# A mixture-of-experts scatter split in two: first rows written plainly with their residual, second rows added

## The chip, the cores and the metric

One NeuronCore of one Trainium2 chip runs the whole program. The metric is the device time of one execution in microseconds (us); the median of three executions is given. The profile is of one more execution. Engines: PE (TensorE), DVE (VectorE), ACT (ScalarE), POOL (GpSimd), and SP, which here only issues DMAs.

## The reference, cut to what matters

All of it is float32. 1072 tokens (16 meta, 1024 prompt, 32 sample) pass a mixer, and then the part that the change touches:

```python
def channel_mixer(x, norm_g, ...):
    n = rms_norm(x, norm_g).reshape(B * T, D)          # x / sigma * g
    return x + hier_moe(n, ...).reshape(B, T, D)

def hier_moe(h, ...):                                  # 4 groups of 8 experts
    # each token: one group, the 2 best experts in it, two gates
    # rows are sorted by expert, in blocks; for each block of one expert e:
    return (silu(xb @ w_gate[e]) * (xb @ w_up[e])) @ w_down[e]
    # out[token] += gate * that row, for both rows of the token
```

An expert has three float32 matrices of 2 MB each (1024 x 512 twice, 512 x 1024), so the 32 experts together read 192 MB from HBM.

## The kernel before

**Stages.** After the attention part come the out-projection with the residual (`xmid`, nine tiles of up to 128 tokens, `wsteps`), the norm of each tile (`norm_scale`: DVE multiplies by 1/sigma and by the gain `gffn`, into `xg`, which SP stores to `n_scr` in HBM), the router in three batches of tiles (`mark`, `shift`, `sum_gates`, `name_gates`, `name_rows`, `place_slots`), and the store of the residual to `y_all`. The router's result is a table `tab` (96 slots x 32 experts, token numbers; an empty slot names a number past the last token, which an indirect DMA skips) and `gtab` (the gates in the same places). They are products of one-hot matrices on PE (`tables`, `last_tables`), with small filler products (`keep_warm`) where PE would stand idle.

**Expert blocks.** Block b is one expert with up to 96 rows (CAP). POOL gathers its rows from `n_scr` into `xg[b % 2]` (`gather`). For b = 0 and 1 PE transposes them and ACT and DVE copy the halves to `xeT` (`block_left`, `block_right`); later blocks are turned by twelve DVE transposes (`turn_rows`). PE makes gate and up products (`gate_up_product`, line 2827), ACT the silu, DVE the product (`hidden`) and its turn (`turn_hidden`), PE the down product (`down_product`). ACT and DVE write gate times product to `yo[b % 2]` (`left_rows`, `right_rows`), and POOL adds the 96 rows to `y_all` with one accumulating indirect DMA (`scatter`). `moved` makes POOL wait until that scatter and the next gather have landed. The last block (expert 23) is scattered in two halves (`scatter_half`). Rows past 96 of an expert would go to further blocks, which run only if there are any (`count_overflow`, `resume_*`, `further_*`).

**Weights.** A ring of 22 halves of 1 MB (`at_half`; half a matrix each) is filled before the blocks start, as the memory of earlier stages comes free. The 22nd, behind the other tensors, is issued once the router's counts are read. From then on SP walks a fixed list (`asked`): `load_behind` waits until PE has used a half of the ring (`s_gp` or `s_dp`), and issues the next half into it. A block uses six halves.

**Order.** Each engine's instructions stand in a fixed order, written out by hand. In `block_pe(b)` PE makes gate and up of b + 1 and then down of b; `block_dve(b)` is `hidden(b+1)`, `right_rows(b)`, `turn_hidden(b+1)`, `turn_rows(b+3)`; `block_act(b)` is `silu(b+1)`, `left_rows(b)`; POOL's round is `gather(b+3)`, `scatter(b)`, `moved(b)`.

Of the kernel before, what the change touches and what calls it, by code (L numbers as in the profile page):

```python
# [93 lines left out]
def hybrid_step(nc, x_prompt, x_sample, cache_k, cache_v, state_pool, page_table, meta_tokens,  # L94
# [167 lines left out]
    at_half = [at + half_size * half for at in at_ring for half in range(2)] + [at_c, at_q + 4 * size]  # L262
# [15 lines left out]
    assert at_x2 == at_half[-1]  # L278
# [17 lines left out]
    xeT.append(tns)  # L296
    assert at <= at_t

    gffn, at = place("gffn", [P, D], F32, at_u)
# [4 lines left out]
    def table(at, limit, shapes):  # L304
# [10 lines left out]
        ("rhs", [P, 2, NB, 2 * NE], F32), ("prod", [P, 2, NB, NE], F32),  # L315
# [5 lines left out]
    def slot_tables(q):  # L321

        lo, n = BATCHES[q][0], BATCHES[q][1] - BATCHES[q][0]
        if q < 2:
            return row_oh[:, :, 0:n, :], rhs[:, :, 0:n, :]
        at = lo - BATCHES[2][0]
        return late_oh[:, :, at:at + n, :], late_rhs[:, :, at:at + n, :]

# [15 lines left out]
    gcol = [gcols[:, i:i + 1] for i in range(2)]  # L344

# [231 lines left out]
    s_lrg = sem("last_rows_gain_ready")  # L577
# [13 lines left out]
    s_gn = sem("last_gates_named_then_counts_read")  # L591
# [63 lines left out]
    tab_ps = bank[0:CAP, 7, 0:2 * NE]  # L655
# [79 lines left out]
    expert_of = list(range(NE))  # L735
    expert_of[NE - 1 - EPG], expert_of[NE - 1] = NE - 1, NE - 1 - EPG
    assert expert_of[NE - 1] // EPG != expert_of[NE - 2] // EPG

    def scatters(b):

        return 16 * (b + 1) if type(b) is int and b < NE - 1 else 16 * (b + 2)

    def copies(b):

        return scatters(b) // 16 if type(b) is int else b + 2
# [69 lines left out]
    def used(b, half):  # L815

        return 8 * b + 4 * half + 4

# [32 lines left out]
    with nc.allow_non_contiguous_dma(reason="small vectors and broadcasts"), blk as block:  # L851

        @block.sync
        def _(sp):
# [177 lines left out]
            sp.dma_start(gffn[:, :], norm_ffn.to_broadcast([P, D])).then_inc(s_wr, 16)  # L1032
# [92 lines left out]
        def _(pool):  # L1125
# [86 lines left out]
            chain.link(pool.memset(lg[:, LAST, :], 0.0))  # L1212
            pool.wait_ge(s_wr, 64)
# [20 lines left out]
            def rows_named(b, further):  # L1234

                return (tab[:, expert_of[b]:expert_of[b] + 1] if b < NE else further[b % 2][:, 0:1]).bitcast(U32)

            def gather(b):
# [3 lines left out]
                if b >= 2:  # L1242
                    pool.wait_ge(s_xt if b < 4 else s_xc, b - 1)
                pool.indirect_dma_start(out=xg[i][0:CAP, :], out_offset=None, in_=n_scr,  # L1244
                                        in_offset=bass.IndirectOffsetOnAxis(ap=rows_named(b, gidx), axis=0),
                                        bounds_check=T - 1, oob_is_err=False).then_inc(s_gl[i], 16)

            def scatter(b):
# [3 lines left out]
                if b >= NE:  # L1252
                    pool.wait_ge(s_sx2, b - NE + 1)
                pool.indirect_dma_start(out=y_all,  # L1254
                                        out_offset=bass.IndirectOffsetOnAxis(ap=rows_named(b, sidx), axis=0),
                                        in_=yo[b % 2][:, :], in_offset=None, compute_op=ALU.add,
# [8 lines left out]
            r = ROWS[LAST]  # L1265
            pool.wait_ge(s_nst[0], 16 * (LAST // 2))
            pool.wait_ge(s_xm, tile_done(LAST))
            xs, gs = [a.rearrange("r (p k) -> r p k", p=P)[:, P // 2:P, :] for a in (xmid[0:r, LAST, :], gffn[0:r, :])]
            pool.tensor_tensor(xg[0][0:r, :].rearrange("r (k p) -> r p k", p=P)[:, P // 2:P, :], xs, gs, ALU.mult).then_inc(s_lrg, 1)
# [7 lines left out]
            gather(2)  # L1277
# [37 lines left out]
        def _(act):  # L1315
# [312 lines left out]
            def root_mid(t):  # L1628
                r, c = ROWS[t], slice(t % 2, t % 2 + 1)
                act.wait_ge(s_ssq2, t + 1)  # L1630
                act.activation(rs[0:r, c], ss[0:r, c], ACT.Sqrt, bias=eps_col[0:r, 0:1],
# [11 lines left out]
            def scale_last_rows():  # L1643

                r = ROWS[LAST]
                act.wait_ge(s_lrg, 1)
                act.wait_ge(s_lg, NT)
                act.activation(xg[0][0:r, :], xg[0][0:r, :], ACT.Copy, scale=rs[0:r, 0:1]).then_inc(s_n2, 1)
# [14 lines left out]
            act.activation(rs[0:r, 0:1], ss[0:r, 0:1], ACT.Sqrt, bias=rest, scale=1.0 / D).then_inc(s_rms2, 1)  # L1663
# [4 lines left out]
            def block_left(b, i):  # L1668
# [6 lines left out]
                act.activation(xeT[i][:, 0:KT // 2, :], xT_ps[:, 0:KT // 2, 0:CAP], ACT.Copy).then_inc(s_xe, 1)  # L1675
# [7 lines left out]
            def left_rows(b, i):  # L1683

                act.wait_ge(s_dp, 8 * b + 8)
                if type(b) is not int:
                    act.wait_ge(s_gc, b - NE + 1)
                gates = gates_of(b, i)
                since(act, s_sc, 16 * b - 16 if type(b) is int else 16 * b)
# [5 lines left out]
            def last_wide_rows(b):  # L1695

                act.wait_ge(s_sc, 16 * b - 16)
# [5 lines left out]
            def first_act():  # L1703
                for b in range(2):
                    block_left(b, b)
                silu(0, 0)

            def block_act(i, b):
                silu(b + 1, 1 - i)
                left_rows(b, i)  # L1710

            def last_act(b):
                if b == NE - 2:
                    silu(b + 1, 1)
                    left_rows(b, 0)
# [15 lines left out]
        def _(dve):  # L1731
# [329 lines left out]

            def place_slots(q):
# [12 lines left out]
            def gain_last(ps):  # L2075

                r = ROWS[LAST]
                return dve.tensor_tensor(xg[0][0:r, :].rearrange("r (k p) -> r p k", p=P)[:, ps, :],
                                         xmid[0:r, LAST, :].rearrange("r (p k) -> r p k", p=P)[:, ps, :],
                                         gffn[0:r, :].rearrange("r (p k) -> r p k", p=P)[:, ps, :], ALU.mult)  # L2080

# [869 lines left out]
```

## Time and profile before

| | |
|---|---|
| median of three executions | 1090.45 us (1090.32 to 1090.7) |
| the profiled execution, its own time | 1091.88 us |
| its span, first to last instruction | 1090.1 us |
| granted TensorE clock, mean | 0.988 of full speed |
| busy: PE, DVE, ACT, POOL | 96%, 50%, 28%, 16% of the span |
| HBM read, written | 272.98 MB, 42.87 MB |

Busy time is an average over stages. The expert blocks run from about 554 us to the end, half of the span. The "DMA" line of the page gives the mean busy share of the 16 DMA engines in 40 slices of 27.25 us; a window's "DMA share" is the same for a chosen stretch.

### The profile page before, as it was taken

To read this page: it belongs to the slowest core of one execution; us is meant where nothing else is said; L and a number is where in the kernel's file an instruction comes from. 1 tells how busy PE (TensorE), PEld (TensorE's weight loads), DVE (VectorE), ACT (ScalarE), POOL (GpSimd) and SP (SyncE) were. 2 spreads that over 40 slices of the span, in tenths; PEclk is the share of its full clock that TensorE was granted. 3 is DMA by queue.
4 is the path that set the end of the run, shared out by engine and by line. 5 is a ranking of instruction groups with operands and counts; after the bars stand their busy time and mean duration, and the time that the engine had idled before them with its cause. 6 is when DMAs were issued, how large, how long until landed. Compare 5 with 4: busy or idle time off the path is not lost.

```text
span 1090.1 us, 29226 instructions
## 1 busy us (share of the span) xinstructions
PE 1045.2 (96%) x12774; PEld 826.0 (76%) x12774; DVE 544.4 (50%) x1052; ACT 309.3 (28%) x592; POOL 174.6 (16%) x160
## 2 busy tenths in 40 slices
PE   8999999999999999999999999999999988898996
PEld 7999999966666549899876898756898556565665
DVE  5327654378875543444734544555455534343431
ACT  6323332266775552222411011101110111101011
POOL 1001200599200000100010111111111111111102
PEclk9999999999999999999989999999999999999999
DMA  7356785000116467767899999999999999999994
GB/s 244 109 166 211 217 272 155 1 13 2 40 31 211 146 232 251 245 220 277 312 351 393 379 383 385 386 383 375 386 379 382 379 390 388 392 390 389 390 389 111
DMA packets 85816, 293.19 MB, mean 269 GB/s; under 512 B 13425, under 2 KB 44849, under 8 KB 60069
## 3 DMA queue, kind: packets, MB, share of 16 engines
q1 hardware_dynamic: 78277, 273.30, 67.2%
q0 software_dynamic: 7280, 17.58, 6.8%
q8 instruction: 103, 1.69, 0.6%
q10 hardware_dynamic: 128, 0.39, 0.1%
q14 instruction: 28, 0.23, 0.1%
HBM read 272.98 MB, written 42.87 MB: 290 GB/s over the span
## 4 chain that ended last, share of the span: by engine, by line
PE 73%; DMA 18%; DVE 4%; SPq 2%; ACT 1%; issue 1%; POOL 0%; ACTq 0%; POOLq 0%
PE bank L2827 20%; DMA w_all<-in_w_up 18%; PE bank L2375 12%; PE bank L2612 8%; PE bank L2418 4%; PE bank L2844 4%; PE bank L2584 3%; PE bank L2547 3%; PE bank L2848 3%; PE bank L2456 3%; SPq L1042 2%; PE bank L2852 2%; DVE keep L1887 1%; PE bank L2693 1%; PE bank L2479 1%
## 5 line engine op out<-in xcount | busy, mean ns | idle before, releaser
L2827 PE MATMUL bank<-w_all,xeT 128*32 128x256 f32 x6144 | 345.6, 382 | 22.2 <-DMA w_all<-in_w_up 19.2
L2827 PEld LDWEIGHTS bank<-w_all,xeT 128*32 128x32 f32 x6144 | 254.4, 111 | 107.0 <-issue 27.9
L2202 DVE STREAM_TRANSPOSE xeT<-xg 32x256 f32<-32x256 f32 x360 | 156.5, 435 | 97.0 <-DMA xg<-n_scr,tab 91.8
L2844 PE MATMUL bank<-w_all,hT 128*32 128x256 f32 x744 | 165.6, 379 | 0.0
L2848 PE MATMUL bank<-w_all,hT 128*32 128x512 f32 x744 | 129.3, 592 | 0.0
L1887 DVE TENSOR_TENSOR_SCAN keep<-keep,unseen 128x1024 f32<-128x1024 f32 (+7 forms) x64 | 94.8, 1514 | 37.8 <-ACT keep L1439 37.7
L2375 PE MATMUL bank<-w_hi,xh 128*128 128x256 f32 x376 | 108.1, 287 | 0.0
L2375 PE MATMUL bank<-w_hi,xl 128*128 128x256 f32 x376 | 105.5, 281 | 0.0
L2375 PE MATMUL bank<-w_lo,xh 128*128 128x256 f32 x376 | 105.5, 280 | 0.0
L2844 PEld LDWEIGHTS bank<-w_all,hT 128*32 128x32 f32 x744 | 81.8, 110 | 30.3
L1681 ACT ACTIVATE sgl<-bank 128x384 f32<-128x384 f32 x32 | 15.7, 490 | 304.2 <-PE bank L2827 304.2
L2612 PE MATMUL bank<-wo_hi,cat 128*128 128x256 f32 (+1 forms) x384 | 89.0, 321 | 0.4 <-issue 0.4
L1254 POOL DMA_INDIRECT out_y_all<-yo,tab x31 | 44.4, 1432 | 204.9 <-ACT yo L1692 199.8
L2852 PE MATMUL bank<-w_all,hT 128*32 128x256 f32 x744 | 76.4, 379 | 0.0
L1244 POOL DMA_INDIRECT xg<-n_scr,tab x32 | 31.5, 986 | 264.4 <-issue 243.3
L2375 PEld LDWEIGHTS bank<-w_hi,xh 128*128 128x128 f32 x376 | 70.8, 188 | 0.6 <-issue 0.2
L2375 PEld LDWEIGHTS bank<-w_hi,xl 128*128 128x128 f32 x376 | 71.1, 189 | 0.0
L2375 PEld LDWEIGHTS bank<-w_lo,xh 128*128 128x128 f32 x376 | 70.8, 188 | 0.0
L2612 PEld LDWEIGHTS bank<-wo_hi,cat 128*128 128x128 f32 x384 | 64.2, 189 | 5.6 <-issue 0.7
L2234 DVE TENSOR_SCALAR yo<-bank,gtab 96x256 f32<-96x256 f32 x31 | 14.9, 480 | 105.3 <-PE bank L2844 105.3
L2215 DVE TENSOR_TENSOR hid<-sgl,bank 128x384 f32<-128x384 f32 x32 | 27.3, 852 | 77.2 <-PE bank L2827 63.3
L1690 ACT ACTIVATE yo<-bank,gtab 96x512 f32<-96x512 f32 x31 | 21.1, 682 | 144.8 <-PE bank L2844 144.8
(307 smaller groups left out, 1505.9 us busy)
## 6 DMA issues: line engine op xcount, KB each, us to landing
w_all<-in_w_down SPq DMA_DIRECT2D x64, 1024.0 KB, 30.2
w_all<-in_w_gate SPq DMA_DIRECT2D x64, 1024.0 KB, 32.6
w_all<-in_w_up SPq DMA_DIRECT2D x64, 1024.0 KB, 8.9
k_scr<-in_cache_k SPq DMA_DIRECT2D x32, 256.0 KB, 3.3
v_scr<-in_cache_v SPq DMA_DIRECT2D x32, 256.0 KB, 3.5
pgk<-k_scr SPq DMA_DIRECT2D x32, 256.0 KB, 3.9
w_raw<-in_w_in SPq DMA_DIRECT2D x7, 1024.0 KB, 7.1
pgv<-v_scr SPq DMA_DIRECT2D x4, 1024.0 KB, 6.6
```

The source lines that it names most:

```text
L1254: pool.indirect_dma_start(out=y_all, out_offset=bass.IndirectOffsetOnAxis(ap=rows_named(b, sidx), axis=0), in_=yo[b % 2][:, :], in_offset= ...
L1887: dve.tensor_tensor_scan(back, back, unseen[:, NK - w:NK][:, ::-1], 1.0, ALU.mult, ALU.max).then_inc(s_p, 1)
L2202: last = dve.transpose(xeT[i][rows_of(s), :, rows_of(g)], lane[:, :, s, :])
L2375: last = pe.matmul(proj_ps(s)[0:r, :], a[:, k, row0(t):row0(t) + r], b[n % 2][:, k, :], start=(k == 0 and j == 0), stop=(k == KT - 1 and j ...
L2418: last = pe.matmul(wide_ps(s)[:, 0:cols], a[n % 2][:, k, c:c + P], b[:, k, lo:lo + cols], start=(k == 0 and j == 0), stop=(k == KT - 1 and ...
L2456: last = pe.matmul(z_ps(a)[:, lo:lo + n], qT[rows, hp, row0(t):row0(t) + P], kT[rows, hp, lo:lo + n], start=True, stop=True)
L2547: last = pe.transpose(t_ps(n)[0:keys, k, :], keep_of(u, a)[:, P * i:P * i + keys], ident[:, :])
L2612: last = pe.matmul(out_ps(s)[0:r, :], cat_tile(a, t)[:, k, 0:r], b[n][:, k, :], start=(k == 0 and j == 0), stop=(k == KT - 1 and j == 2))
L2827: lasts = [pe.matmul(pair_ps(i)[rows_of(q), g, :, :], xeT[i][:, k, rows_of(g)], pair_of(b, i, k, q), start=(k == 0 and g != 1), stop=(k == ...
L2844: return pe.matmul(y_right_ps(g), hT[:, ft, rows_of(g)], w[ft // 2][:, ft % 2, DA:D], start=first and g != 1, stop=ends, skip_group_check= ...
L2848: pe.matmul(y_left_ps[rows_of(g), :], hT[:, ft, rows_of(g)], w[ft // 2][:, ft % 2, 0:512], start=first, stop=ends, skip_group_check=True)
L2852: lasts = [pe.matmul(y_mid_ps[rows_of(g), :], hT[:, ft, rows_of(g)], w[ft // 2][:, ft % 2, 512:DA], start=first, stop=ends, skip_group_che ...
```

## The change

Each token has two expert rows. The one whose expert stands first in the order of the blocks is now written to `y_all` plainly, by a DMA without accumulation, with the token's residual inside; the second is added as before. For that:

- `norm_scale` no longer applies the gain, so that `n_scr` holds x / sigma. The gain is applied when the rows have been turned: by ACT and DVE in the copies of blocks 0 and 1, and by eight ACT instructions per later block (`gains`). The DVE and POOL instructions that put the gain on the last tile (`gain_last` and one of POOL) go.
- sigma is kept (`sig`), and a third table `wtab` holds sigma in the slots of first rows and 0 in those of second rows (`name_residuals` on DVE, `residual_tables` on PE, `result_tables` on DVE). `result_tables` also makes the two lists of tokens, `tab_first` and `tab_later`.
- `keep_rows` (ACT) writes wtab times the gathered row to the block's result buffer, which is x for a first row and 0 for a second; `add_rows` (DVE, five instructions that read it and PSUM) takes the place of `left_rows` and `right_rows`.
- Each block up to the 31st has two indirect DMAs of 96 slots, one for each list. There are three result buffers; the third lies where the 22nd half of the ring was, so the ring has 21 halves.
- `gather` runs one block further ahead (b + 4), and waits for `keep_rows` of two blocks before. Expert 31 moves to its natural place; 23 stays last.
- 14 fillers before the first block become 8, the residual products, and 4.

```diff
-    at_half = [at + half_size * half for at in at_ring for half in range(2)] + [at_c, at_q + 4 * size]
+    at_half = [at + half_size * half for at in at_ring for half in range(2)] + [at_c]
...
+    yo.append(place("yo2", [CAP, D], F32, at_x2)[0])
+    NY = len(yo)
...
-            sp.wait_ge(s_gn, 2)
-            b, j, half = halves[2 * NWS + 1]
-            load_half(j, expert_of[b], b, b % 2, half)
...
+                if 2 <= b < NE:
+                    pool.wait_ge(s_ya, b - 1)
...
+                else:
+                    pool.indirect_dma_start(out=y_all,
+                                            out_offset=bass.IndirectOffsetOnAxis(ap=column(tab_first, b), axis=0),
+                                            in_=results_of(b), in_offset=None,
+                                            bounds_check=T - 1, oob_is_err=False).then_inc(s_sc, 16)
...
             for b in range(NE - 1):
-                if b + 3 < NE:
-                    gather(b + 3)
+                if b + 4 < NE:
+                    gather(b + 4)
                 scatter(b)
...
-                act.activation(xeT[i][:, 0:KT // 2, :], xT_ps[:, 0:KT // 2, 0:CAP], ACT.Copy).then_inc(s_xe, 1)
+                for k in range(KT // 2):
+                    last = act.activation(xeT[i][:, k, :], xT_ps[:, k, 0:CAP], ACT.Copy, scale=gain_p[:, k:k + 1])
+                last.then_inc(s_xe, 1)
+
+            def gains(b, i):
+
+                act.wait_ge(s_xc, b + 1)
+                for k in range(KT):
+                    last = act.activation(xeT[i][:, k, :], xeT[i][:, k, :], ACT.Copy, scale=gain_p[:, k:k + 1])
+                last.then_inc(s_xe, 1)
+
+            def keep_rows(b, i):
+
+                act.wait_ge(s_gl[i], 16 * (b // 2 + 1))
+                if b < NY:
+                    act.wait_ge(s_tab, 1)
+                else:
+                    act.wait_ge(s_sc, scatters(b - NY))
+                act.activation(results_of(b).rearrange("r (p k) -> r p k", p=P), xg[i][0:CAP, :].rearrange("r (k p) -> r p k", p=P),
+                               ACT.Copy, scale=wtab[:, expert_of[b]:expert_of[b] + 1]).then_inc(s_ya, 1)
...
             def first_act():
                 for b in range(2):
                     block_left(b, b)
+                for b in range(2):
+                    keep_rows(b, b)
                 silu(0, 0)
+                gains(2, 0)
 
             def block_act(i, b):
                 silu(b + 1, 1 - i)
-                left_rows(b, i)
+                if b + 2 < NE - 1:
+                    keep_rows(b + 2, i)
+                if b + 3 < NE:
+                    gains(b + 3, 1 - i)
...
+            def add_rows(b, i):
+                dve.wait_ge(s_dp, 8 * b + 8)
+                dve.wait_ge(s_ya, b + 1)
...
+                add(slice(0, CAP), slice(0, 512), y_left_ps)
+                add(slice(0, CAP), slice(512, DA), y_mid_ps)
+                for g in range(LANES):
+                    last = add(rows_of(g), slice(DA, D), y_right_ps(g))
+                last.then_inc(s_yd, 1)
...
                 for b in range(2):
                     block_right(b, b)
+                result_tables()
                 count_overflow()
...
-            keep_warm(14)
+            keep_warm(8)
+            pe.wait_ge(s_gn, 3)
+            residual_tables()
+            keep_warm(4)
```

## Rows read from the trace of the kernel before

**Rows 1.** The page: DMA busy tenths in 40 slices of 27.25 us.
```profile
DMA  7356785000116467767899999999999999999994
```
**Rows 2.** Windows: busy us of PE, PEld, DVE, ACT, POOL; PEclk, DMA share, GB/s.
```profile
545.00:552.00 7.00, 7.00 (x38) 6.87 (x38) 1.06 (x4) 0.00 (x0) 2.56 (x4) 0.53 0.71 241
552.00:560.00 8.00, 7.70 (x119) 5.85 (x118) 0.56 (x1) 0.49 (x1) 1.00 (x1) 0.99 1.02 419
...
750.00:800.00 50.00, 50.00 (x852) 39.30 (x847) 23.82 (x50) 7.30 (x14) 8.16 (x7) 1.00 1.02 384
...
850.00:900.00 50.00, 43.27 (x706) 26.95 (x698) 22.70 (x48) 6.12 (x12) 5.79 (x5) 1.00 1.02 385
```
**Rows 3.** The chain that ended last: start us, us, what.
```profile
548.13 5.29 PE bank L2769 x28
...
554.38 5.39 PE bank L2827 x96
...
581.44 10.36 PE bank L2827 x192
...
814.53 10.14 PE bank L2827 x188
...
1060.65 10.57 PE bank L2827 x192
```
**Rows 4.** SP's DMA issues around the first release: start us, us.
```profile
549.72 0.81 SPq L1042 DMA_DIRECT2D w_all<-in_w_down  x1
559.88 0.33 SPq L1042 DMA_DIRECT2D w_all<-in_w_gate  x1
```
**Rows 5.** All 192 weight loads (line 1042), issue to landing.
```profile
DMA to landing us min/median/max: 5.9/31.3/35.7
```
**Rows 6.** DMA queues, packets, MB, share: 728:734, 759:764, then 598:602 us.
```profile
q0 software_dynamic: 112, 0.36, 30.0%
...
q0 software_dynamic: 112, 0.21, 21.2%
...
q1 hardware_dynamic: 178, 1.29, 87.7%
q0 software_dynamic: 112, 0.20, 15.9%
```
**Rows 7.** DMA queues: ACT's queue (q10) in 536:543, the loads' (q1) in 538:539 us.
```profile
q10 hardware_dynamic: 128, 0.39, 14.1%
...
q1 hardware_dynamic: 34, 0.26, 62.8%
```
**Rows 8.** The page: the queue of POOL's DMAs over the whole span.
```profile
q0 software_dynamic: 7280, 17.58, 6.8%
```
**Rows 9.** Timeline of DVE: start us, us, instruction, idle before it.
```profile
548.24 0.19 DVE L2163 COPY gtab<-bank 96x32 f32<-96x32 f32 x1 [2.33 <-PE bank L2749]
...
564.32 0.17 DVE L2176 CAST ovmi<-ovm 1x23 int32<-1x23 f32 x1
...
581.56 0.48 DVE L2234 TENSOR_SCALAR yo<-bank,gtab 96x256 f32<-96x256 f32 x1 [3.74 <-PE bank L2844]
```
**Rows 10.** Timeline of ACT.
```profile
535.16 1.15 ACT L1648 ACTIVATE xg<-xg,rs 48x1024 f32<-48x1024 f32 x1 [0.85 <-DVE lg L2109]
...
553.79 0.49 ACT L1675 ACTIVATE xeT<-bank 128x384 f32<-128x384 f32 x1 [10.10 <-PE bank L2800]
...
581.56 0.68 ACT L1690 ACTIVATE yo<-bank,gtab 96x512 f32<-96x512 f32 x1 [4.67 <-PE bank L2844]
582.26 0.95 ACT L1692 ACTIVATE yo<-bank,gtab 32x256 f32<-32x256 f32 x2
```
**Rows 11.** Groups: busy us, mean ns, idle before and what ended it.
```profile
L2202 DVE STREAM_TRANSPOSE xeT<-xg 32x256 f32<-32x256 f32 x360 | 156.5, 435 | 97.0 <-DMA xg<-n_scr,tab 91.8
```
**Rows 12.** Timeline of POOL at the end: line 1254 `scatter`, line 1295 `scatter_half`.
```profile
1078.99 1.40 POOL L1254 DMA_INDIRECT out_y_all<-yo,tab  x1 [14.39 <-ACT yo L1692]
...
1083.09 1.40 POOL L1295 DMA_INDIRECT out_y_all<-yo,lidx  x1 [0.55 <-issue]
```

More of the change, by code:

```diff
@@ L1276, in _ @@
                 pool.tensor_scalar(lidx[:, part:part + 1], tab[:, e:e + 1], 2.0, float(part), ALU.mult, ALU.add).then_inc(s_ln, 1)
-            gather(2)
+            for b in range(2, 4):
+                gather(b)
             pool.wait_ge(s_yst, 16 * LAST)
@@ L1662, in _ @@
             act.wait_ge(s_ssq2, NT)
-            act.activation(rs[0:r, 0:1], ss[0:r, 0:1], ACT.Sqrt, bias=rest, scale=1.0 / D).then_inc(s_rms2, 1)
+            act.activation(sig[0:r, LAST:NT], ss[0:r, 0:1], ACT.Sqrt, bias=rest, scale=1.0 / D).then_inc(s_rms2, 1)
             act.dma_start(y_all[row0(LAST):T, :], xmid[0:ROWS[LAST], LAST, :]).then_inc(s_yl, 16)
@@ L1714, in last_act @@
                     silu(b + 1, 1)
-                    left_rows(b, 0)
                 else:
@@ L2060, in name_rows, with name_residuals @@
                 chain.done(dve.tensor_tensor(slot_tables(q)[1][:, :, :, 0:NE], ek[:, :, 0:n, :], rows, ALU.mult))
+            def name_residuals(q):
+                lo, hi = BATCHES[q]
+                ts, n = slice(lo, hi), hi - lo
+                if q == 2:
+                    dve.wait_ge(s_tbp, 2)
+                places = tmp32[:, 0:n, 0:2 * EPG].rearrange("p t (k e) -> p k t e", k=2)
+                numbers = io_row[:, 0:EPG].rearrange("p (x y e) -> p x y e", x=1, y=1).to_broadcast([P, 2, n, EPG])
+                chain.link(dve.tensor_tensor(places, oh[:, :, ts, :], numbers, ALU.mult))
+                chain.link(dve.reduce_sum(turn[:, :, ts], places, axis=AXX))
+                for k in range(2):
+                    chain.done(dve.tensor_tensor(weight[:, k, ts], turn[:, k, ts], turn[:, 1 - k, ts], ALU.is_lt))
+                chain.settle()
+                chain.link(dve.tensor_tensor(weight[:, :, ts], weight[:, :, ts],
+                                             sig[:, ts].rearrange("p (x t) -> p x t", x=1).to_broadcast([P, 2, n]), ALU.mult))
+                return dve.tensor_tensor(residual_table(q), ek[:, :, 0:n, :], each(weight[:, :, ts], NE), ALU.mult)
             def place_slots(q):
@@ L2146, in _ @@
                         chain.done(name_gates(q))
+                        chain.done(name_residuals(q))
                         name_rows(q)
@@ L2259, in block_dve @@
                 hidden(b + 1, 1 - i)
-                right_rows(b, i)
+                add_rows(b, i)
                 turn_hidden(b + 1)
@@ L2268, in last_dve @@
                     turn_hidden(b + 1)
-                    right_rows(b, 0)
+                    add_rows(b, 0)
                 else:
@@ L2751, in last_tables, with residual_tables @@
                 last.then_inc(s_tbp, 1)
+            def residual_tables():
+                lo, hi = BATCHES[2]
+                one_hot = slot_tables(2)[0]
+                for t in range(lo, hi):
+                    r = ROWS[t]
+                    for k in range(2):
+                        last = pe.matmul(tab_ps[:, 2 * NE:3 * NE], one_hot[0:r, k, t - lo, :], late_res[0:r, k, t - lo, :],
+                                         start=False, stop=(t == LAST and k == 1), skip_group_check=True)
+                last.then_inc(s_tbp, 1)
             for s in range(2, len(wsteps) - 2):
```

116 lines of the change are left out of this document (61 added, 55 removed).

## The prediction, made before the changed kernel was run

> **What bounds the kernel now.** I read the page first. Its DMA line stands at 9 tenths from the 20th slice, about 545 us, to the 39th [rows 1], so the half of the span that the expert blocks fill might be bound by transfers. The windows say when. In 750 to 800 us PE is busy throughout and the DMA share is 1.02; in 850 to 900 the share is the same and PE is busy 43.27 of 50 us [rows 2]. The chain of waits gives the two regimes. Its gate-and-up stretches of 10.36 us start every 15.54 us from 581.44 to 814.53 (233.09 us for 15 blocks); at that pace the stretch of block 31 would start at 581.44 + 29 x 15.54 = 1032 us. It starts at 1060.65 [rows 3]. So PE waits for 29 us in all after 830 us, and the end is set by the weight stream, which is full from about 550 us on. What takes time from the 16 DMA engines delays the end one for one, early or late in the stage; what takes time from PE, DVE or ACT does so only if it leaves the DMA engines without work. That can happen in one place. A load that finds the queue empty lands 5.9 us after its issue, the median one after 31.3 [rows 5]: later a deep queue stands before the engines. At the start there is none: the last load of the filling (the 22nd half) is issued at 549.72, the next at 559.88, when PE has used the first half [rows 4], and four 1 MB loads and a gather just fill the time between (share 1.02 in 552 to 560 [rows 2]).
>
> So the sum has four terms: DMA time saved, the later first release, the missing 22nd half, and the tail after the last load.
>
> **Saved by plain rows.** In two windows that each hold one scatter of 112 packets (96 slots and 16 completions), queue 0 moved 0.36 MB at 30.0% of 6 us and 0.21 MB at 21.2% of 5 us [rows 6]. Times 16 engines these are 28.8 and 17.0 engine-us for 88 and 51 rows of 4 KB; the difference gives 0.32 engine-us for an accumulated row, and some 0.4 is left for the 24 or 61 other packets, 0.007 to 0.017 each; I take 0.012. The trace before has no plain scatter. The nearest rows are ACT's stores of 96 rows of 4 KB from SBUF to HBM, beside the weight stream on another queue: 0.39 MB at 14.1% of 7 us, 15.8 engine-us, 0.165 a row. They also take no more than that: while they hold the rest, the loads have 62.8% and move 0.26 MB in a microsecond [rows 7], which is 62% of the 0.42 (419 GB/s) that they move alone in 552 to 560 [rows 2]. The other bound is a gathered row: 15.9% of 4 us for 49 rows is 0.21, and the loads beside it slow down too (1.29 MB in 4 us [rows 6], where 1.68 would pass alone: the missing 0.39 MB are 14.9 engine-us, 0.30 a row). A scatter writes as ACT's store does and doesn't read HBM, so I take 0.165, with 0.30 as the bound. The 17.58 MB of queue 0 [rows 8] are 4292 rows, which is both rows of all 1072 tokens gathered and scattered, so 1072 rows become plain: 1072 x (0.32 - 0.165) / 16 = 10.4 us. Against it stand 31 more DMAs of 112 packets: 3472 x 0.012 / 16 = 2.6 us. Net -7.8 us; bounds: -11 (the packets free) and +1.3 (a plain row at 0.30).
>
> The Trainium skill has two rules that would change this term. "DMA: Bandwidth & Descriptors", section "Where 436 GB/s comes from", says that between HBM and SBUF the HBM side binds, at about 358 GB/s. The windows move 384 and 385 GB/s with both directions counted once [rows 2], so this trace doesn't show that ceiling. By the rule the term would be bytes alone, 4.39 MB less read: an estimate of 12.3 us, and a sum of -4.6. (1072 rows of 4 KB at the 385 GB/s of the rows would be 11.4.) The section "Bandwidth" of the same page calls transfers under 64 KB descriptor-dominated and gives a floor of 0.67 us of DMA time for 64 packets; by that a further DMA in each of 31 blocks would cost an estimated 20.8 us and the sum would be +18 or more. The trace leaves 0.4 engine-us for 61 small packets [rows 6] and speaks against it.
>
> **The first release.** Three edits lie on PE's way to the first gate-and-up product. (1) Before, 14 fillers take 5.29 us, 0.378 each [rows 3]. After, 12 fillers and six products of the residual table stand there: 4.5 us and, by the products they resemble, nearly 2; part of it runs after the clock has risen from the 0.53 of 545 to 552 us [rows 2], so +1.0 us, bounds 0.5 and 1.3. `name_residuals` on DVE (six instructions of at most 0.36 us) is covered by the 2.33 us in which DVE waited for PE [rows 9], and by the 8 fillers; without that cover it costs up to 1.5. (2) The tables have 96 columns for 64 in the batches before the last: +0.3 at most. (3) ACT copies the left half of block 0 in four instructions with a scale, not one of 0.49 us. With a scale, 512 columns take 0.68 and 256 take 0.475 [rows 10], so 96 take about 0.34, four 1.36: +0.9. DVE's copy stays one instruction. Sum 2.2 us, first release at about 562.1; bounds 1.0 and 3.5. `norm_scale` without its second operand and the dropped `gain_last` pay for `name_residuals(1)` on DVE, and PE sets the pace there; I count nothing, and up to 0.7 if they don't cover it, inside the bounds.
>
> **The missing half.** From 550 us three loads of 2.5 us each remain (1.05 MB at 419 GB/s [rows 2]), so the engines run dry at about 558. At the release 171 loads remain instead of 170: +2.6 us. Gathers 2 and 3, which filled the gap before, move behind the first releases, whose pairs are 6 us apart for 5 us of loads: +0.5 of further dry time. So the stream runs 2.2 + 2.6 + 0.5 = 5.3 us late; bounds 3.5 and 8.
>
> Is more late at block 2? `keep_rows(0)` waits for `s_tab`, whose last instruction moves from 564.5 [rows 9] by 2.2 us and by the seven small ones of `result_tables` (1.2) to 567.9. Behind it on ACT are `keep_rows(1)`, the first silu and `gains(2)`; on POOL gather 2 waits for it, with gather 3 behind. An ACT instruction of 1024 columns takes 1.15 us [rows 10], up to twice that read with a stride, so gather 2 is issued at 569 to 570 and lands some 5 to 8 us later; 12 turns of 0.435 [rows 11] and 8 gains of 0.34 end at 582 to 586. PE wants them at 581.44 + 2.2 = 583.6. By then ten loads were released and some 8 us of them wait, so a stall up to about 2.5 us costs nothing; I count 0.
>
> **Later blocks.** With t = 0 at the end of a down product, DVE adds (0.69 + 0.48 + three of 0.48 = 2.6 us, from 0.48 for 256 columns [rows 9] and ACT's 0.68 for 512), turns the hidden rows (0.6) and then block b + 3 (5.2): 8.4; the gains end at 11.2, and PE wants them at 15.5. DVE loses the 91.8 us it waited for gathers [rows 11], since each is now issued a block earlier; that was not on the path and gives nothing. Behind the gains on ACT stands the silu, due at 10.4, 0.9 late; its product is wanted 5 us later. Cover gone, a block would cost what the gains exceed 4.3 us.
>
> **The tail.** The last scatters are a chain on POOL: line 1254 starts at 1078.99 when ACT is done, and 1083.09 is the second half of the last block [rows 12]. After, `add_rows(30)` takes 2.6 us for ACT's 1.63 [rows 10], +0.9, and one more DMA stands in the row at 1.40 + 0.5 = 1.9; the slack of 0.4 us that the halves had goes: +2.4 us, bounds 1.5 and 3.
>
> **The sum.** 5.3 - 7.8 + 2.4 = -0.1 us. Against the profiled execution's 1091.88 (span 1090.1) that is 1091.8; its own time is 1.43 above the median of 1090.45, so the median after would be 1090.3. The measurement tells 0.2%, 2.2 us, from no change.
>
> **The rivals.**
> - *A wash* (the sum above, 1088.3 to 1092.6): chance 0.40.
> - *The start hides more.* If the slip is 1 us and the queue refills without the dry time: 3.5 - 9.5 + 1.5 = -4.5, 1086. For it: the bounds of each term, and that packets skipped may cost less than 0.012. Against: four terms would all have to lean one way. 0.20.
> - *Only bytes set the stream's pace.* A second read of HBM costs its bytes and a skipped packet nothing: 5.3 - 11.4 + 2.4 = -3.7, 1086.7. For it: the loads are bound by something at 385 to 419 GB/s [rows 2]. Against: ACT's stores, which read no HBM, slowed the loads by their full share [rows 7]. 0.08. (The first rule of the Trainium skill above says this.)
> - *A plain row costs what a gathered one takes*, 0.30: the term is +1.3, the whole +9, 1099.5. It decides from 0.20 a row upwards, where the sum passes +2.2. For it: both are POOL's DMAs; against: ACT's store takes 0.165 and an accumulated row slows nobody beyond its own time. 0.13.
> - *Block 2 late.* Gather 2 behind `keep_rows(0)` lands past 578, PE stalls over 2.5 us and stops the releases while the queue is short: +3 to +4, 1094. 0.12.
> - *The clock.* PE waits 1.4 us for ACT just before the first product, and it ran at 1.2 GHz in 545 to 552 us [rows 2] after gaps. At that level again for the first product, the release comes 2.5 to 5 us later: 1094. 0.05.
> - *A POOL DMA costs the engines more than its packets.* If the 4.7 engine-us by which the gather's window lost more than its share [rows 6] belong to the DMA and not to its rows, 31 more are +9, 1099.5. Against it: the accumulating windows leave no such rest. 0.02. (By the second rule of the Trainium skill above it would be an estimated +18.)
>
> Faster 0.28, within 0.2% 0.40, slower 0.32. The range 1085.5 to 1096 leaves out the gathered price and the costly DMA, and a little below. The likeliest case's own range is 1088.3 to 1092.6.
>
> **What would show it.** Queue 0: 10,750 packets, its share of the engines down from 6.8% to about 6.1. First gate-and-up product at 554.38 [rows 3] + 2.2 = 556.6, first release at 562; a DMA share well under 1 between 558 and 563. Block period 15.54 until the stream runs out, then the last gate-and-up stretch at about 1058. POOL's last DMA 25 us behind the start of that stretch, not 22.4. The prediction is wrong if a plain row holds an engine for more than 0.2 us, if PE stalls between 580 and 600, or if the gains hold PE in every block.

## The result and the profile after

The changed kernel takes 1103.62 us (median of 4 runs, 1102.77 to 1105.94) against 1090.38 for the kernel before beside it: a ratio of 1.0126, 95% interval 1.0108 to 1.0143. It is 13.2 us slower. The prediction was 1090.3, range 1085.5 to 1096: wrong, and outside the range.

The profiled execution took 1102.77 us, span 1101.0. Its page (its head, the DMA line over 40 slices, queue 0, and the chain that ended last):
```profile
span 1101.0 us, 29605 instructions
...
DMA  7356784000126368676999999999999999999961
...
q0 software_dynamic: 10752, 17.60, 6.1%
...
DMA 15%; ACT 3%; issue 3%; POOL 2%; PE 2%; another core or an unknown queue 0%; POOLq 0%; DVE 0%; ACTq 0%
```
Queue 0 came as predicted: 10,752 packets, and its share fell from 6.8% [rows 8] to 6.1%, which is 74.1 to 67.2 us. So the DMA engines did get back 7 us. But the last digits of the DMA line say that they ran out of work earlier than before, although the kernel ends later: 6 and 1 stand in the last two slices, for 9 and 4 [rows 1]. And in place of PE and the loads of `in_w_up` [rows 3], the chain that ended last is made of `out_y_all<-yo,tab_later`, the landing of the second scatter.

The chain in order of time (start us, us, what) shows one turn of a cycle, from one landing to the next:
```profile
843.37 11.41 DMA out_y_all<-yo,tab_later
...
854.87 2.18 ACT yo L1714
...
857.93 0.44 POOL xg L1262
...
859.22 0.95 POOL out_y_all L1273
860.17 0.30 issue
860.47 11.39 DMA out_y_all<-yo,tab_later
```
L1714 is `keep_rows`, L1262 a gather, L1273 the first scatter. Read it as a loop through three engines. `keep_rows(b+2)` on ACT needs the third buffer back, so it waits until scatter(b-1) has landed: 11.4 us from its start on POOL. The gather of b+4 needs the rows that `keep_rows(b+2)` reads out of `xg`: 2.2 us. scatter(b) stands behind that gather in POOL's list: 0.54 of issue, 0.44 and 0.53 of gather, 0.3 of issue, 0.95 of first scatter, 0.3. Then scatter(b) has to land. From the turn at 826.02 to that at 1048.88 us there are 13 in the chain, 17.14 us each (222.86 us in all); PE needs 15.54 for a block [rows 3]. The table of waits (engine line waited for: us in total, times, longest) has the same pair at its head:
```profile
POOL xg L1262 <- ACT yo L1714: 345.5, 27, 19.5
ACT yo L1714 <- DMA out_y_all<-yo,tab_later: 252.1, 27, 13.4
```
The end of the chain shows what the last block waited for:
```profile
1048.88 11.47 DMA out_y_all<-yo,tab_later
...
1060.44 0.28 ACT yo L1714
1060.71 1.78 issue
1062.49 2.23 ACT xeT L1704 x8
...
1064.76 10.56 PE bank L2914 x190
...
1089.19 1.41 POOL out_y_all L1315
```
Before, the last gate-and-up stretch started at 1060.65 when a load landed [rows 3]; here it starts 4.1 us later when ACT's gains (L1704) are done, which stand behind the last `keep_rows`. No load is waited for. The rest of the 10.9 us of span is behind that start: POOL's last DMA comes 24.4 us after it (22.4 before [rows 3, 12]), and the span ends 11.8 us after the start of that DMA, for 7.0.

The start is not what the prediction made of it. Windows (busy PE, PEld, DVE, ACT, POOL, granted clock, DMA share, GB/s):
```profile
545.00:552.00 7.00, 5.17 (x54) 4.61 (x56) 0.56 (x1) 1.03 (x4) 1.02 (x3) 1.00 0.97 307
552.00:560.00 8.00, 8.00 (x147) 5.37 (x140) 2.19 (x10) 1.03 (x4) 0.00 (x0) 1.00 0.78 286
...
570.00:580.00 10.00, 8.46 (x136) 4.80 (x124) 5.36 (x13) 0.78 (x3) 0.00 (x0) 1.00 1.02 346
580.00:600.00 20.00, 18.34 (x275) 13.70 (x279) 9.85 (x21) 8.62 (x18) 4.40 (x4) 0.91 0.96 366
```
TensorE was granted its full 2.4 GHz in 545 to 552, where it had 0.53 before [rows 2], and the first gate-and-up product came at 551.40, 3 us earlier than before and not 2.2 later. The engines still ran dry in 552 to 560 (0.78 for 1.02). And PE, which was busy throughout 570 to 580 before, stood still for some 3 us ahead of block 2's products; they waited for its gains until 581.4. That stall cost more than its own length: behind it the granted clock fell to 0.91 of full in 580 to 600, part of it at the 1.2 GHz level, and block 2's 192 gate-and-up products took 13.2 us for the 10.6 of the kernel before.

### The profile page after: what moved, and what is told of

It reads as the page before. It is cut to its first block and busy times, and to the rows that moved or that the text cites. A ratio compares the mean times of both kernels' runs of the same rounds, so it can differ in the third digit from the quotient of the medians.

```text
span 1101.0 us, 29605 instructions
## 1 busy us (share of the span) xinstructions
PE 1058.4 (96%) x12782; PEld 844.6 (77%) x12782; DVE 585.8 (53%) x1166; ACT 392.0 (36%) x776; POOL 205.4 (19%) x191
## 3 DMA queue, kind: packets, MB, share of 16 engines
q0 software_dynamic: 10752, 17.60, 6.1%
## 5 line engine op out<-in xcount | busy, mean ns | idle before, releaser
L2914 PE MATMUL bank<-w_all,xeT 128*32 128x256 f32 x6144 | 363.7, 381 | 12.9 <-ACT xeT L1704 6.8
L2914 PEld LDWEIGHTS bank<-w_all,xeT 128*32 128x32 f32 x6144 | 270.8, 110 | 96.8 <-issue 29.2
L2931 PE MATMUL bank<-w_all,hT 128*32 128x256 f32 x744 | 166.3, 379 | 0.0
L1714 ACT ACTIVATE yo<-xg,wtab 96x1024 f32<-96x1024 f32 x31 | 67.1, 2167 | 256.0 <-DMA out_y_all<-yo,tab_later 252.1
L2935 PE MATMUL bank<-w_all,hT 128*32 128x512 f32 x744 | 145.3, 592 | 0.3 <-issue 0.3
L1262 POOL DMA_INDIRECT xg<-n_scr,tab x32 | 31.8, 995 | 480.8 <-ACT yo L1714 345.5
L2302 DVE SCALAR_TENSOR_TENSOR yo<-bank,gtab,yo 32x256 f32<-32x256 f32 (+2 forms) x155 | 80.2, 533 | 70.3 <-PE bank L2931 68.9
L1704 ACT ACTIVATE xeT<-xeT,gain_p 128x96 f32<-128x96 f32 x240 | 66.8, 361 | 88.5 <-DVE xeT L2262 83.1
L2939 PE MATMUL bank<-w_all,hT 128*32 128x256 f32 x744 | 93.7, 379 | 0.0
L1567 ACT ACTIVATE qsum<-bank,one_col 128x512 f32<-128x512 f32 (+3 forms) x85 | 51.4, 644 | 31.9 <-PE bank L2620 31.3
```

The source lines that it names most:

```text
L1567: act.activation(dst, src, ACT.Identity, bias=one_col[0:keys, 0:1], scale=-1.0).then_inc(s_te, 1)
L1704: last = act.activation(xeT[i][:, k, :], xeT[i][:, k, :], ACT.Copy, scale=gain_p[:, k:k + 1])
L1714: act.activation(results_of(b).rearrange("r (p k) -> r p k", p=P), xg[i][0:CAP, :].rearrange("r (k p) -> r p k", p=P), ACT.Copy, scale=wta ...
L2302: return dve.scalar_tensor_tensor(out=out, in0=product, scalar=gates[rows, :], in1=out, op0=ALU.mult, op1=ALU.add)
L2914: lasts = [pe.matmul(pair_ps(i)[rows_of(q), g, :, :], xeT[i][:, k, rows_of(g)], pair_of(b, i, k, q), start=(k == 0 and g != 1), stop=(k == ...
L2931: return pe.matmul(y_right_ps(g), hT[:, ft, rows_of(g)], w[ft // 2][:, ft % 2, DA:D], start=first and g != 1, stop=ends, skip_group_check= ...
```

## The experiments

Each is set beside runs of the kernel before on the same chip. The chips differ: experiments 1 to 3 ran on one, 4 to 6 on a second, 7 and 8 on a third, 9 on a fourth, so kernels of different groups are best compared by their distance from the kernel before. First, the loop: three theories stood against each other, the cycle of waits, DMA engines that gained nothing, and the late start.

**1. POOL scatters first, then gathers.**
```
             for b in range(NE - 1):
+                scatter(b)
                 if b + 4 < NE:
                     gather(b + 4)
-                scatter(b)
```


> The changed kernel with POOL's round turned: the two scatters of block b are issued before the gather of block b + 4, not behind it. Theory 1 (a cycle of waits sets the pace): after the change the scatter of b has to land before keep_rows of b + 3, keep_rows before the next gather, and the gather stands before the next scatter on POOL; 11.5 us of landing + 2.2 of keep_rows + 3.4 on POOL make the 17.1 us per block of the chain of waits. With the scatter in front the cycle no longer passes keep_rows, the period falls to PE's 15.5 until the loads run out, and the time falls by 5 to 9 us, to about 1096. Theory 2 (the DMA engines, still at share 1.02, set the pace, and the plain rows saved nothing): the order on POOL changes no byte, the time stays within 1.5 us of the changed kernel's 1103.6.

Measured: 1095.18 us (10 runs), 1.0041 of before [1.0026, 1.0056]. ACT's wait for the later scatter falls from 252.1 to 75.8 us, POOL's for ACT from 345.5 to 19.3, and POOL's timeline (start us, us, instruction, idle before it) keeps PE's pace of 15.54:
```profile
695.93 0.95 POOL L1273 DMA_INDIRECT out_y_all<-yo,tab_first  x1 [11.55 <-DVE yo L2302]
697.18 1.45 POOL L1277 DMA_INDIRECT out_y_all<-yo,tab_later  x1 [0.30 <-issue]
698.94 0.99 POOL L1262 DMA_INDIRECT xg<-n_scr,tab  x1 [0.30 <-issue]
711.47 0.95 POOL L1273 DMA_INDIRECT out_y_all<-yo,tab_first  x1 [11.54 <-DVE yo L2302]
```
The order on POOL is the only edit. Against the 1103.62 of the changed kernel it is worth 8.4 us, but that kernel ran on another occasion and, as experiment 9 shows, some 2 us of its time were something else. By the distance from the kernel before it is worth about 6.4 us: 4.3 here, 10.7 for the changed kernel in experiment 9.

**2. A shorter step in the cycle.** The rows are copied in the order in which they lie; the output's columns come out permuted.
```
-act.activation(results_of(b).rearrange("r (p k) -> r p k", p=P), xg[i][0:CAP, :].rearrange("r (k p) -> r p k", p=P),
+act.activation(results_of(b), xg[i][0:CAP, :],
```


> The changed kernel with keep_rows copying the gathered row in the order in which it lies (1024 columns in sequence, no stride on either side); the residual then goes to permuted columns, so the first rows of y are not the reference's. Nothing else changes. Theory 1 (the cycle): the ACT instruction of 2.17 us becomes one of about 1.15, the cycle is 1 us shorter, the period falls from 17.1 to about 16.1 us; over the 27 blocks that run in the cycle that is far more than the loads allow, so the time falls until the loads bind, by 4 to 8 us. Theory 2 (DMA engines): no change within 1.5 us.

Measured: 1090.80 us (10 runs), ratio 0.9997 [0.998, 1.0013], more than expected. The copy takes 1.15 us instead of 2.16. POOL's runs of DMAs around 700 us are still ordered by the cycle, 16.5 and 15.8 us apart:
```profile
683.14 0.99 POOL L1262 DMA_INDIRECT xg<-n_scr,tab  x1 [12.78 <-ACT yo L1714]
...
699.67 0.99 POOL L1262 DMA_INDIRECT xg<-n_scr,tab  x1 [12.52 <-issue]
...
715.43 0.99 POOL L1262 DMA_INDIRECT xg<-n_scr,tab  x1 [11.77 <-ACT yo L1714]
```
A cycle half a microsecond longer than a block only eats the lead of the gathers, and the loads set the pace from about 830 us on anyway; one that is 1.6 longer eats three times as much in each block, and then holds PE. The measure is what the loads allow: in the kernel before, PE comes from block 2 to block 31 in 479.2 us, 16.5 a block [rows 3]. A loop of 16.1 stays under that, one of 17.1 doesn't. So 1.0 us off a step was worth over 10 (10.8 by the distance from the kernel before).

Experiment 2 still has the loop, experiment 1 has none, and yet experiment 2 is 4.4 us faster, on the same chip and with intervals that don't touch. The loads' own queue shows where most of that lies (600 to 1050 us: packets, MB, share of 16 engines; first experiment 1, then 2):
```profile
q1 hardware_dynamic: 21912, 159.57, 89.0%
```
```profile
q1 hardware_dynamic: 22042, 160.52, 88.8%
```
A megabyte of weights holds the engines for 2.51 us in experiment 1 and for 2.49 in experiment 2; over the 181 MB of the stage that is 3.7 us. The same split runs through all the profiles: 2.48 to 2.50 where POOL gathers first, 2.51 where it scatters first. Breaking the loop by order has this price; what in the order makes it is not shown.

**3. The missing half alone.** The kernel before with a ring of 21 halves.
```
-    at_half = [... for half in range(2)] + [at_c, at_q + 4 * size]
+    at_half = [... for half in range(2)] + [at_c]
```


> The kernel before with a ring of 21 halves: the 22nd half is neither placed nor loaded. By the prediction's step the stream is one load later: DMA engines dry for 2 to 3 us before the first release, time +2.6 to +3.1 us against before. Rival: the stream catches up since PE, not the loads, sets the pace until 830 us: below 1 us.

Measured: 1091.74 us against 1090.89, ratio 1.0008 [0.9993, 1.0024]: 0.9 us, at most 2.6, and nothing at all is within the interval. The engines did run dry (share in the last but one column):
```profile
552.00:560.00 8.00, 7.91 (x140) 5.44 (x144) 2.00 (x6) 1.66 (x2) 1.84 (x2) 1.00 0.73 262
```
That is 2.3 us of missing share, of which the end shows 0.9.

**4. Block 2 on time.** Experiment 1 with the result tables and the overflow count between DVE's two block copies. (There is no measurement with the copied rows released before the count: result buffer 0 lies over the count's temporaries.)
```
-                for b in range(2):
-                    block_right(b, b)
+                block_right(0, 0)
                 result_tables()
                 count_overflow()
+                block_right(1, 1)
```


> The scatter-first kernel (1095.2 us), in which DVE also makes the result tables and counts the overflow between its two block copies, where it sat idle for 6.4 us, instead of behind them. The first copied rows, and with them the gathers of blocks 2 and 3, come about 4.8 us earlier. If the stall of 4 to 5 us ahead of block 2's products is what leaves the DMA engines dry (4.7 us of missing share between 552 and 600 us in the scatter-first kernel), PE does not stall between 570 and 585, the share of 580 to 600 rises from 0.89 to about 1.0, and the time falls by 2 to 4 us, to 1091 to 1093, about the kernel before. Rival: the dry time comes from the start alone (the 22nd half and the gathers moved behind the first releases); then the stall goes but the share of 552 to 570 stays as it is, and the time falls by less than 1 us.

Measured: 1092.99 us (10 runs), 1.0024 [1.0009, 1.0039]; 2.2 us less than experiment 1, on another chip and with intervals that overlap. PE is busy in all of 560 to 600, at full clock, and the share of 580 to 600 is 1.02. Experiment 1 had in its place (clock 0.85, share 0.89)
```profile
580.00:600.00 20.00, 19.34 (x285) 10.44 (x288) 10.54 (x22) 7.77 (x15) 3.45 (x3) 0.85 0.89 344
```
The missing share is 2.6 us, so that block 2's stall was worth some 2 us is likely, and not clear of the noise. In 552 to 560 the share is 0.54: the dry time of the missing half stays.

**5. Plain against accumulated rows.** Experiment 4 with `compute_op=ALU.add` on the first scatter too; the residual counts twice.

> The kernel with the tables between the copies, in which the first scatter of a block accumulates too, as the second does (so the residual is counted twice in the output). It has the same waits, the same number of POOL DMAs and the same packets; the 1072 rows written plainly are accumulated. If the DMA engines set the pace and a plain row saves what the prediction took (0.32 less 0.165 engine-us), it is 10.4 us slower than the kernel with plain rows, and queue 0's share is about 1 point higher. Rival: a plain row costs the engines as much as an accumulated one, or the pace is set by bytes of the loads alone; then it is within 2 us.

**6. One more POOL DMA a block that moves nothing.** The kernel before with this behind each whole scatter, where `away` holds 96 names past the last row:
```
+                    pool.indirect_dma_start(out=y_all, out_offset=bass.IndirectOffsetOnAxis(ap=away[:, 0:1].bitcast(U32), axis=0),
+                                            in_=yo[b % 2][:, :], in_offset=None, compute_op=ALU.add,
+                                            bounds_check=T - 1, oob_is_err=False).then_inc(s_sc, 16)
```


> The kernel before, with a second accumulating scatter behind each of the 31 whole ones whose 96 names are all past the last row, so that it writes nothing. It prices one more POOL DMA per block and the longer end. By the prediction's 0.012 engine-us for a skipped packet: 2.6 us of DMA time, and 1.7 us more on POOL ahead of the last two scatters. If the longer end of the changed kernel (10.4 us from the start of the last scatter's end to the end of the span, 5.6 before) comes from the number of POOL's DMAs, another 1.4 us or more: 1094.5 to 1097 in all. Rivals: a further DMA costs the engines more than its packets, by which 31 of them are 9 us or more, over 1102; or it costs nothing, within 1 us of the kernel before.

Measured, on one chip with experiment 4: accumulating everything 1098.83 us, 5.8 more than with plain rows; the empty scatters 1094.47, 3.9 more than the kernel before [1.0022, 1.0043]. Queue 0 on the three pages (experiments 4, 5, 6; spans 1091.4, 1096.8, 1091.2):
```profile
q0 software_dynamic: 10752, 17.60, 6.0%
```
```profile
q0 software_dynamic: 10752, 17.61, 6.9%
```
```profile
q0 software_dynamic: 10752, 17.61, 7.0%
```
65.5, 75.7 and 76.4 us (a tenth of a point is 1.1 us). Making 1072 rows plain saves 10.2 us of the engines, where the prediction worked out 10.4; 3472 empty packets cost 2.3 over the 74.1 of before, where it had 2.6. Not all of it reaches the end: the last gate-and-up stretch comes 6.3 us earlier with plain rows (1057.11 for 1063.41). Of the 3.9 us between, 2.9 lie at the start of these two executions, by chance or not: the DMA share in 552 to 600 is 0.93 with plain rows and 0.99 without.

**7. The tables alone, in the changed kernel,** whose POOL order stays.

> The changed kernel with one edit: the result tables and the count between DVE's two block copies. POOL's order stays, so the cycle of waits (later scatter landed, copied rows, gather, first scatter) stays too. If the cycle sets the pace at 17.1 us a block, only its start moves, by the 2 to 4 us that block 2 comes earlier: 1099.5 to 1102 us, and the period between later scatters stays 17.1. Rival: the late block 2 is what costs the 13 us, by the queue that runs dry at the start; then the time falls to 1093 or less.

**8. Rows in natural order everywhere,** on top of experiment 4: norm, copy and both kinds of turns.
```
-lane = xg[i][rows_of(g), :].rearrange("r (k s c) -> r k s c", k=KT, s=QUARTERS)
+lane = xg[i][rows_of(g), :].rearrange("r (s c k) -> r k s c", k=KT, s=QUARTERS)
```


> The kernel with the scatter first and the tables between the copies (1093.0 us), in which the normed rows lie in scratch and in SBUF in their natural order: the row norm, the copy of the residual rows by ACT, the DVE turns and PE's turns of blocks 0 and 1 read or write them so, and the output is the same. ACT's copy of 1024 columns takes 1.15 us instead of 2.16. If these microseconds of ACT cost time beside the cycle of waits (the kernel with rows in order alone took 1090.8 us, the one with the scatter first alone 1095.2), it takes 1088 to 1091, as fast as the kernel before or faster. Rival: with the cycle gone ACT is off every path that sets the time, and it stays at 1093; if DVE's turns with a stride take longer than 0.435 us, it is slower.

Measured, both on one chip: 1105.53 us for 7 (four runs from 1099.8 to 1110.4) and 1104.70 for 8. Neither fits its theory: 8 has experiment 1's order and no cycle, and yet its POOL DMAs are 16.8 us apart. Something else was at work. In 698 to 715 us of experiment 8 PE's weight loads (the second x of each row) thin out for 2 us, with full clock and no wait:
```profile
698.00:705.50 7.50, 7.50 (x141) 6.94 (x135) 5.65 (x11) 1.15 (x1) 1.94 (x2) 1.00 1.01 404
705.50:707.50 2.00, 1.94 (x21) 0.57 (x14) 1.96 (x4) 0.00 (x0) 1.44 (x2) 1.00 1.05 426
707.50:715.00 7.50, 7.42 (x119) 6.70 (x122) 3.99 (x6) 3.51 (x10) 0.00 (x0) 1.00 1.02 359
```
14 in 2 us, where 36 would go by the rate of the row above. The changed kernel's profile has the same in 705 to 707 (x13). Both have it in nearly every block, 2.3 us (changed kernel: 2.8) after POOL's first DMA of the block; experiments 1, 2 and 4 have it in none, nor has the profile of the kernel before. So three kernels were run again side by side on a fourth chip.

**9. Three kernels again.**

> The changed kernel itself, beside two of its variants on one chip, since three kernels (this one, the one with early tables alone, the one with rows in natural order) show something in every block that the others do not: about 1.5 us in which PE, inside the gate-and-up product, issues only three weight loads where it issues 28 otherwise, 2.3 us after POOL starts its run of DMAs. If the cycle of waits alone makes the changed kernel slow, it takes 1101 to 1105 us here too, with or without the pauses, and the period between its later scatters is 17.1. If the pauses are what costs, and belong to this order of work, they are here again and the time is the same 1101 to 1105. If the pauses belong to the chip and not to the kernel, this run, on another chip, may lack them; it then tells what the cycle costs by itself: 1096 or less if little, 1100 or more if it is the cause.

> The kernel with the scatter first and the tables between the copies, again, beside the changed kernel on one chip. It took 1093.0 us without pauses. If pauses belong to an order of work, it has none and takes 1092 to 1094; if they belong to the chip, it has them here exactly when the changed kernel beside it has them, and takes 1.2 us or more per paced block longer, over 1100.

> The kernel with rows in natural order, again, beside the other two. It took 1104.7 us with pauses in every block. If DVE's strided turns (0.636 us for 0.433, 2.4 us a block) make it slow, it takes 1102 or more here as well, at a period of 16.8 us; if the pauses do and they belong to the chip, it takes 1090 to 1094 where they are absent.

Measured: the changed kernel 1101.36 us (ratio 1.0099 [1.0082, 1.0116]), experiment 4's kernel 1092.73 (1.0022 [1.001, 1.0033]), the natural order 1094.38 (1.0048 [1.0029, 1.0067]). The pauses are gone from all three, so the kernel alone doesn't make them. The chip alone doesn't seem to either: beside experiments 7 and 8 the kernel before took 1090.65 us, as on every other chip. They cost experiment 8's kernel 10 us, and the changed one about 2. The natural order, whose copy on ACT takes 1.15 us like experiment 2's, is not faster than experiment 4's kernel (its turns on DVE are slower): once the loop is gone, that microsecond of ACT buys nothing. Without the pauses the changed kernel's cycle is there as it was:
```profile
1034.68 11.48 DMA out_y_all<-yo,tab_later
...
1046.24 2.18 ACT yo L1714
...
1049.31 0.44 POOL xg L1262
...
1050.61 0.95 POOL out_y_all L1273
...
1051.86 11.72 DMA out_y_all<-yo,tab_later
```
17.18 us from the start of one later scatter to the next. PE keeps its 15.54 for the first blocks, while the gathers still have a lead, and is held from about 750 us on. Beside it, the kernel of experiment 4, whose last gate-and-up stretch waits for a load and starts 10.5 us earlier (the rows of the last stretch, first of the changed kernel, then of the other):
```profile
1067.99 10.57 PE bank L2914 x192
```
```profile
1057.50 10.36 PE bank L2914 x192
```
Experiment 7 stays unreadable: with pauses in every block it can't say what the early tables do alone.

## Why the prediction was wrong

**The step that failed is "Later blocks", which counted 0.** It costed what DVE and ACT do in a block (8.4 and 11.2 us of 15.5) and said that each gather "is now issued a block earlier", as a gain without a price. It never followed what that gather waits for. Three edits that look harmless alone close a loop: `keep_rows` needs a buffer that a scatter must leave, the gather needs `keep_rows`, and POOL's list puts the next scatter behind the gather. Rows of the kernel before would not have been enough to see that it binds. The trace of before has a landing for the scatter, beside the same full queue (from its start on POOL):
```profile
DMA to landing us min/median/max: 4.5/9.1/10.1
```
With 9.1 us the loop would be 14.8 us long, under the 15.54 of a block. It is 17.14 because the landing became 11.4 (11.5 in experiment 9): the later scatter is now the third DMA that POOL issues in a row. Experiment 1 moves the gather to the third place, and the figures change sides: the gather lands after 11.0 us (8.7 in experiment 2), the later scatter after 9.7. Experiment 1 breaks the loop by order alone (6.4 us by the distance from the kernel before), experiment 2 shortens one step (10.8 us), and on the fourth chip, side by side, breaking it and bringing block 2 forward gives 8.6. None of the rivals had this mechanism either. Some 2 us of the 13.2 measured first are not the loop's but the pauses' (experiment 9).

The other steps, in the prediction's order:
- *Saved by plain rows*, -7.8: right in the engines' time (experiments 5 and 6; the rival of a plain row at the gather's 0.30 falls). By the prediction's own terms its lower bound, with free packets, is -10.4 and not -11. The floor that the Trainium skill gives for small DMAs ("DMA: Bandwidth & Descriptors", section "Bandwidth"), from which the prediction drew +18, falls too: 31 empty ones cost 3.9 us in all. What was off is the premise that the end moves one for one: it moved by 5.8 us (medians) for 10.2 of engine time. That an accumulated row costs more agrees with the Trainium skill ("Collectives: The Full Stack", section "Stop ④ — SDMA + CCE: where bytes move and the add happens", where a reducing descriptor reads two streams and writes one). That the second read is the reason, no run here shows.
- *The first release*, +2.2: came 3 us earlier. The added work was there, but the clock before the first product was the full one in this execution; the profiles of the experiments have 0.60 to 1.00 in the same window. One profile's clock is no base for a term of this size.
- *The missing half*, +2.6 and 0.5: the half alone costs 0.9 by experiment 3 (-0.8 to 2.6), so probably over-sized; the 0.5 for the moved gathers was not measured by itself.
- *Block 2*, counted 0: PE stood for 3.05 us where 2.5 were allowed, and then ran slower, which the prediction had nowhere; together some 2 us (experiment 4), not clear of the noise. The rival "block 2 late" (0.12) was right as a part.
- *The tail*, +2.4: under-sized. This table takes the start of the last gate-and-up stretch, POOL's last DMA behind it and the end of the span behind that (us):
```
                         stretch   last DMA   end
before                   1060.65    +22.4     +7.0
before, empty scatters   1059.44    +23.5     +8.3
all rows accumulated     1063.41    +24.5     +8.9
experiment 4             1057.11    +24.1    +10.3
experiment 4, again      1057.50    +23.8    +10.1
changed, again           1067.99    +24.1    +10.0
```
Each row is one execution, and its first gate-and-up product came anywhere from 550.2 to 554.4 us, so a microsecond or two in the first column is chance; the other two columns repeat better. From before to experiment 4 the tail grew by 4.8 us, 1.6 of it in front of the last DMA (predicted 2.4) and 3.2 behind it, where the prediction had nothing. Of the end, some 1.3 come with a second POOL DMA per block, and 1.3 more with plain ones. The latter stands in POOL's closing DRAIN instruction, 7.97 us in every profile with plain rows and 6.3 to 6.6 in those without; what it does stays open.

So with the loop broken and block 2 on time, the two profiled executions differ like this: the last stretch starts 3.5 us earlier, the tail is 4.8 longer, and the span grows by 1.3. By the medians the kernel is 2.4 us slower than before on one chip and 2.1 on the other (1.0024 and 1.0022). That is near the wash that was predicted for the change as a whole, partly by luck: two costs that the prediction didn't have, the 3.2 us behind the last DMA and the slower loads of the new order, stand against terms that it took too large. No version tried here beats the kernel before; what is left against it is the tail and those loads.

## What to carry to other kernels

When an edit makes an instruction wait, write out the whole loop that it closes, engine by engine, with the landing time of every DMA in it, and compare its length to the period of a block. Take the landing time for the place where the DMA will stand: behind two others it was 11.4 us here, where 9.1 had been measured before, and that made the difference. A queue's order is an edge of that loop like any semaphore: a gather that must wait should not stand in front of a scatter that is ready. And before a difference of some microseconds in every block is explained by the code, run the same kernel on another chip.

## What the hardware showed

- An accumulating indirect DMA of POOL ends on the engine's timeline after 1.45 us, and lands beside the full weight stream 9.1 us after its start in the kernel before, 9.7 as the second of three DMAs in a row (experiment 1), and 11.4 as the third. The Trainium skill ("Perfetto Trace Analysis", section "DMA Instruction — SWDGE (GPSIMD)") says that the profiler's end of such an instruction is the last descriptor written and not the data moved, and the trace agrees. Who costs a wait by that bar is off by a factor of six to eight.
- On POOL a plain indirect scatter of 96 slots takes 0.95 us, an accumulating one 1.45. On the 16 engines an accumulated row of 4 KB costs 0.15 engine-us more than a plain one (experiment 5), and a row that is skipped about 0.01 (experiment 6).
- The order in which POOL issues its DMAs changed how long the same loads held the engines: 2.51 us per MB with the scatters first, 2.49 with the gather first. The cause is open.
- A stall of 3 us ahead of block 2 cost more than 3 us: the granted clock fell to the 1.2 GHz level behind it (0.84 to 0.91 as the mean of 580 to 600), and the next 192 products took 12.2 to 13.3 us for 10.6.
- ACT copies 96 x 1024 in 1.15 us in order and in 2.16 with a step of 128 elements; DVE's transposes go from 0.433 to 0.636 us when their source has a step of 8. The Trainium skill ("SBUF — State Buffer", section "Door 1: The DMA port swizzle") puts a penalty on each access that crosses to a new line of 16 bytes, and both fit: each of these steps leaves the line.
- PE can lose some 1.5 us in every block to pauses that no wait and no granted clock shows. The same kernel had them on one chip and not on another, and the kernel before shows no sign of them on either. Their cause is open.
